# A three-layer float32 block on one core: earlier weight splits, rotary partners in partition halves, and a half-spectrum Fourier transform

## The chip, the cores and the metric

One core of one Trainium2 chip runs the whole program. The metric is the device time of one execution in microseconds, here the median of several runs.

## The reference

The input is x (1 x 512 x 1024, float32). The first layer projects the normed x into many parts and runs two attentions side by side: a sparse one (an indexer scores all earlier keys, the best 128 of each query are kept, softmax over those) and one with a forget gate. Both are gated and projected, merged by sigmoid weights and added to x. Then comes an "even" layer and an "odd" layer, both modulated by a condition vector, the first also over 256 context rows. The parts that the change touches are these:

```
def axial_rope(x, row, col):            # even layer: queries and keys, heads of 2 x 32 features
    half = x.shape[-1] // 2; nf = half // 2
    def rotate(u, pos):
        ang = pos[:, None] * inv_freq
        u1, u2 = u[..., :nf], u[..., nf:]
        return concatenate([u1 * cos - u2 * sin, u2 * cos + u1 * sin], axis=-1)
    return concatenate([rotate(x[..., :half], row), rotate(x[..., half:], col)], axis=-1)

def fourier_mix(u):                     # odd layer: 8 groups of 64 features
    ug = u.reshape(B, N, 8, 64)
    return fft2(ug, axes=(1, 3), norm='ortho').real.reshape(B, N, 512)
```

## The kernel before

The activations lie with features on the partitions, 128 of them by 512 tokens. Each operand of a large product is split into a high part (cast to fp32r) and a low part, and each product is made of three: high x high, high x low, low x high. The weights come as a stream of units (128 x 512) in granules of four (1 MB). SyncE loads a granule into one of two raw buffers (`w_raw`, line 1347) and, before it loads the next into the same buffer, waits until both parts of the old one exist. ScalarE casts each unit to its high part (`high(u)`, line 1371), in an order written out by hand: `high(upto)` casts all units up to that one, and waits for each until TensorE has read the unit that lay in the same place (there are four places, `ROOM`). GpSimd subtracts to get the low part (line 1194). TensorE waits for both (`tiles`, line 645). `ahead(chunk)` casts up to three units past the end of a chunk. Every engine runs its own program in order, so a wait holds back all that stands behind it.

The eight PSUM banks are dealt out by a pool: `next_bank` takes the next bank of the current tuple `pool[0]` and waits until its last reader has given it back. Small guest products (`modulate`, line 715) and their turned rows (`turn_due`, line 729) take banks in the same way; VectorE's `modulation` (line 2232) reads and frees the latter.

The stages that the change touches, in order of time:

- **keys, qi, qa (14 to 79 us).** After the keys' two tiles are copied, ScalarE computes the forget gate (lines 1456 to 1464: Abs, Exp, Ln with table loads and waits for VectorE), and only then goes on with `ahead("qi")`. After qi and qa it copies the four qa tiles (line 1469) and then splits the first index query (`prep_i(0)`: ScalarE line 1425, VectorE line 2122), for which the first index score (line 784) waits.
- **ga, gb, vb (135 to 219 us).** VectorE picks the best 128 keys in 16 rounds of `max` and `match_replace` (lines 2175, 2178), then frees gb's banks in `gated("gb")` (line 2165), then runs `modulation(0, (0, 1))`. The banks of gb are 5, 6, 7 and 4; its guest takes 2 and its turned row 3. The pool of vb is (0, 1, 2, 5, 6, 7), so vb's fourth tile takes bank 5.
- **After the attention, mb0, mb1 (349 to 403 us).** ScalarE casts the attention results (lines 1591, 1595) with one or more `high` between each two, runs the eight sigmoids of the merge gate (line 1599), and then the sigmoids that free mb0's banks (line 1606), the first of which mb1's third tile needs.
- **The even layer's queries and keys (632 to 709 us).** The partner of each feature is made by a permutation product (`rotate`, line 773, eight products in plain float32) between the units of e_v; VectorE's `rope` multiplies by the cosine (line 2086), the PSUM partner by the sine (line 2088) and adds (line 2090), in the order query 0, key 0, query 1, key 1 and so on. SyncE then stacks the parts of each head by 24 copies inside SBUF for the first two heads (line 1257), and `score_even` (line 987) waits for them.
- **The Fourier part (1299 to 1345 us).** The product with the sequence transform (`dft`) gives cosine columns 0 to 256 and sine columns 1 to 255. ScalarE copies each tile in two pieces (lines 1965, 1966), VectorE mirrors both (lines 2583, 2584), and TensorE applies the feature transform to two full tiles of 512 columns for each of four j, adding in PSUM (lines 1165, 1166). VectorE multiplies by the gate (line 2589), ScalarE and VectorE split the result, ScalarE waits for all of it (`nix_lo` 8), issues four loads of x (lines 1973, 1974) and only then casts the fifth unit of oo0.

## Time and profile before

| what | value |
|---|---|
| median of 3 runs (lowest to highest) | 1370.41 us (1368.09 to 1373.72) |
| the profiled execution's own time | 1370.77 us |
| its span, first to last instruction | 1369.0 us |
| TensorE / VectorE / ScalarE / GpSimd busy | 94% / 49% / 45% / 34% |
| mean granted TensorE clock | 0.983 of full |
| chain that ended last, by engine | PE 72%, DVE 11%, ACT 8% |

Busy shares are averages over the span. The times of an order in time are from the span's start; "[4.47 <-POOL w_low L1194]" says that the engine sat idle for 4.47 us before this row until that instruction released it. "x4" merges four instructions into one row.

### The profile page before, as it was taken

To read this page: it belongs to the slowest core of one execution; us is meant where nothing else is said; L and a number is where in the kernel's file an instruction comes from. 1 tells how busy PE (TensorE), PEld (TensorE's weight loads), DVE (VectorE), ACT (ScalarE), POOL (GpSimd) and SP (SyncE) were. 2 spreads that over 40 slices of the span, in tenths; PEclk is the share of its full clock that TensorE was granted. 3 is DMA by queue.
4 is the path that set the end of the run, shared out by engine and by line. 5 is a ranking of instruction groups with operands and counts; after the bars stand their busy time and mean duration, and the time that the engine had idled before them with its cause. 6 is when DMAs were issued, how large, how long until landed. Compare 5 with 4: busy or idle time off the path is not lost.

```text
span 1369.0 us, 19570 instructions
## 1 busy us (share of the span) xinstructions
PE 1286.5 (94%) x7164; PEld 1001.5 (73%) x7164; DVE 672.0 (49%) x1279; ACT 622.8 (45%) x1336; POOL 459.3 (34%) x360
## 2 busy tenths in 40 slices
PE   7899999999999998869999999999988999999998
PEld 6677766676678776668777887787867878677776
DVE  4466974665503342273268668623704601565343
ACT  7434325655432334262146666645325422655533
POOL 4534343221343443360133333331351133231341
PEclk9999999999999999989999999999999999999999
DMA  6331442000441544341052430001153232121452
GB/s 222 101 100 62 147 161 93 32 32 32 139 154 62 207 189 158 123 160 41 31 152 73 107 101 32 32 32 63 62 200 113 87 127 89 62 93 62 154 148 68
DMA packets 28685, 140.46 MB, mean 103 GB/s; under 512 B 4304, under 2 KB 5968, under 8 KB 15984
## 3 DMA queue, kind: packets, MB, share of 16 engines
q1 hardware_dynamic: 21840, 117.85, 25.5%
q10 hardware_dynamic: 6752, 21.35, 4.7%
q8 instruction: 60, 0.98, 0.3%
q14 instruction: 33, 0.27, 0.1%
HBM read 122.87 MB, written 6.29 MB: 94 GB/s over the span
## 4 chain that ended last, share of the span: by engine, by line
PE 72%; DVE 11%; ACT 8%; issue 3%; DMA 3%; POOL 3%; ACTq 1%; DVEq 0%; POOLq 0%; SPq 0%
PE psum L645 46%; PE psum L673 5%; DMA w_raw<-stream 2%; PE psum L784 2%; POOL w_low L1194 2%; DVE arena L2178 2%; PE psum L1011 2%; PE psum L1179 2%; DVE small L2175 2%; PE psum L875 2%; ACT w_high L1371 2%; PE psum L633 1%; PE psum L995 1%; DVE arena L2028 1%; PE psum L861 1%
## 5 line engine op out<-in xcount | busy, mean ns | idle before, releaser
L1194 POOL TENSOR_TENSOR w_low<-w_raw,w_high 128x512 fp32r<-128x512 f32 x264 | 353.4, 1352 | 733.2 <-ACT w_high L1371 733.0
L1371 ACT CAST w_high<-w_raw 128x512 fp32r<-128x512 f32 x264 | 158.1, 621 | 335.5 <-PE psum L645 183.7
L645 PE MATMUL psum<-x_high,w_high 128*128 128x512 f32 x528 | 224.5, 425 | 13.3 <-POOL w_low L1194 6.8
L645 PE MATMUL psum<-x_low,w_high 128*128 128x512 f32 x528 | 209.8, 397 | 0.0
L645 PE MATMUL psum<-x_high,w_low 128*128 128x512 f32 x528 | 209.6, 397 | 0.0
L645 PEld LDWEIGHTS psum<-x_high,w_high 128*128 128x128 f32 x528 | 99.9, 189 | 59.1 <-issue 23.8
L645 PE MATMUL psum<-w_high,x_high 128*128 128x512 f32 x288 | 120.0, 417 | 14.7 <-ACT w_high L1371 6.2
L645 PEld LDWEIGHTS psum<-x_high,w_low 128*128 128x128 f32 x528 | 99.9, 189 | 24.1
L645 PE MATMUL psum<-w_low,x_high 128*128 128x512 f32 x288 | 115.4, 401 | 0.0
L645 PE MATMUL psum<-w_high,x_low 128*128 128x512 f32 x288 | 115.2, 400 | 0.0
L645 PEld LDWEIGHTS psum<-x_low,w_high 128*128 128x128 f32 x528 | 100.3, 190 | 17.8 <-issue 0.7
L645 PEld LDWEIGHTS psum<-w_high,x_high 128*128 128x128 f32 x288 | 55.3, 192 | 40.1 <-issue 15.8
L2404 DVE TENSOR_REDUCE small<-psum 128x1 f32<-128x768 f32 (+1 forms) x96 | 69.9, 770 | 19.7 <-PE psum L987 19.6
L1731 ACT ACTIVATE arena<-psum,small 128x768 f32<-128x768 f32 (+1 forms) x84 | 63.3, 761 | 16.8 <-DVE small L2404 16.6
L1740 ACT COPY arena<-psum 128x512 f32<-128x512 f32 (+1 forms) x80 | 36.7, 459 | 68.2 <-PE psum L995 67.5
L1223 POOL TENSOR_SCALAR arena<-arena,small 128x768 f32<-128x768 f32 (+1 forms) x48 | 40.3, 840 | 79.1 <-DVE small L2411 79.1
L645 PEld LDWEIGHTS psum<-w_high,x_low 128*128 128x128 f32 x288 | 55.0, 191 | 13.6
L645 PEld LDWEIGHTS psum<-w_low,x_high 128*128 128x128 f32 x288 | 55.4, 192 | 12.9 <-issue 1.0
L673 PE MATMUL psum<-x_high,w_high 128*128 128x512 f32 x96 | 42.2, 440 | 0.5 <-DVE arena L2397 0.5
L2416 DVE SCALAR_TENSOR_TENSOR arena<-arena,small 128x768 f32<-128x768 f32 (+1 forms) x36 | 30.1, 835 | 18.9 <-POOL arena L1223 18.9
L673 PE MATMUL psum<-x_high,w_low 128*128 128x512 f32 x96 | 37.9, 395 | 0.0
L673 PE MATMUL psum<-x_low,w_high 128*128 128x512 f32 x96 | 37.9, 395 | 0.0
(456 smaller groups left out, 2688.5 us busy)
## 6 DMA issues: line engine op xcount, KB each, us to landing
w_raw<-stream SPq DMA_DIRECT2D x98, 1024.0 KB, 4.9
x_kept<-arena ACTq DMA_DIRECT2D x8, 512.0 KB, 4.5
arena<-x_kept ACTq DMA_DIRECT2D x8, 512.0 KB, 5.7
arena<-bias ACTq DMA_DIRECT2D x8, 512.0 KB, 3.7
q_masked<-e_q_high SPq DMA_DIRECT2D x24, 96.0 KB, 2.2
arena<-x SPq DMA_DIRECT2D x4, 512.0 KB, 5.2
arena<-x ACTq DMA_DIRECT2D x4, 512.0 KB, 7.4
arena<-ctx ACTq DMA_DIRECT2D x4, 512.0 KB, 6.8
```

Of the source, the lines that this page charges most:

```text
L645: mm = pe.matmul(o, l, r, start=(first and n == 0 and kind != "fc"), stop=(last and n == len(passes) - 1))
L673: mm = pe.matmul(o, l, r, start=k == 0 and n == 0, stop=k == NK - 1 and n == 2)
L784: mm = pe.matmul(acc, q[rows, :], k[rows, :], start=n == 0, stop=not more and n == 2)
L875: mm = pe.matmul(acc[64 * hh:64 * hh + 64, 0:P], v, A_PT[:, 2 * (d % 2) + hh, P * kt:P * kt + P], start=kt == 0, stop=kt == t)
L1011: mm = pe.matmul(acc[64 * hh:64 * hh + 64, 0:P], E_V[:, kt, 64 * head:64 * head + 64], E_PT[:, 2 * (d % 2) + hh, P * kt:P * kt + P], start ...
L1194: pool.tensor_tensor(PLACE[u][1], RAW[:, g % 2, u % 4, :], PLACE[u][0].bitcast(F32), ALU.subtract).then_inc(w_lo, 1)
L1223: pool.tensor_scalar(second, second, SM[:, RINV + c + 1:RINV + c + 2], SM[:, 82:83], ALU.mult, ALU.mult)\
L1371: act.copy(PLACE[u][0], RAW[:, g % 2, u % 4, :]).then_inc(w_hi, 1)
L1731: frees(act.activation(map_place(s, m), PS[:, 512 * b:512 * b + w], ACT.Exp, bias=scr(NEGMAX + c), accum_out=scr(ROWSUM + c)), key)
L1740: frees(act.copy(E_PT[:, 2 * (d % 2) + hh, P * c:P * c + w], ps[:, 0:w]), key)
L2404: dve.tensor_reduce(scr(NEGMAX + 2 * (s % 4) + m), PS[:, 512 * b:512 * b + w], AX.X, ALU.max, negate=True).then_inc(sig("e_neg"), 1)
L2416: dve.scalar_tensor_tensor(e0, e0, scr(RINV + c), e1, ALU.mult, ALU.add).then_inc(sig("e_p"), 1)
```

## The change

In the first layer ScalarE's splits are put in another order, `modulation(0, (0,))` moves into VectorE's selection loop and one pool changes. In the even layer the weight columns of e_q and e_k are laid out anew so that a feature and its partner lie 64 partitions apart; the permutation products go, VectorE makes the partner by two multiplications of 64 partitions each that write to the other half, all queries come before all keys, and the 96 stacking copies read every fourth partition instead of 32 neighbours. In the odd layer the feature transform is applied to 257 and 255 columns, each in its own part of a bank, and the sum and the mirror come after it.

```
-SQ = {n: i for i, n in enumerate(("ident", "causal", "perm_a", "perm_e", "ones_blk", "dft_c", "dft_s"))}
+SQ = {n: i for i, n in enumerate(("ident", "causal", "ones_blk", "dft_c", "dft_s"))}
...
+    for n in ("e_q", "e_k"):
+        chunks[n] = chunks[n].reshape(D, 4, 2, 2, 2, 2, 8).transpose(0, 1, 5, 4, 6, 2, 3).reshape(D, 512)
...
-        ROPE_E = [(t, (c, j)) for j in range(4) for t, c in ((E_Q[:, j, 0:S], "e_q"), (E_KF[:, j, :], "e_k"))]
+        ROPE_E = [(t[:, j, 0:S], (c, j)) for t, c in ((E_Q, "e_q"), (E_KF, "e_k")) for j in range(4)]
...
-        N_F = arena(4096, 8, S)
+        N_F = arena(4096, 4, S)
+        N_T = arena(6144, 4, S)
+        N_ODD = TAB.rearrange("p a (b n) -> p (a b) n", b=2)
```

On TensorE:

```
-            pool[0] = (0, 1, 2, 5, 6, 7)
+            pool[0] = (0, 1, 2, 3, 5, 6)
             gemm("vb", X)
...
                 unit("e_v", k, X, C)
-                if k < 4:
-                    pool[0] = (3, 0)
-                    rotate("rope_e", ROPE_E[2 * k:2 * k + 2], "perm_e", 2 * k)
...
             for j in range(4):
-                pe.wait_ge(sig("dft_whole"), j + 1)
+                consumed(pe, ("dft", j))
                 acc = next_bank(("fmix", j))
-                pe.matmul(acc[:, :], square("dft_c"), N_F[:, j, :], start=True, stop=False)
-                fills_bank(pe.matmul(acc[:, :], square("dft_s"), N_F[:, 4 + j, :], start=False, stop=True),
+                pe.matmul(acc[:, 0:HALF + 1], square("dft_c"), N_F[:, j, 0:HALF + 1], start=True, stop=True)
+                fills_bank(pe.matmul(acc[:, HALF + 1:S], square("dft_s"), N_F[:, j, HALF + 1:S], start=True, stop=True),
```

On SyncE:

```
-                    rows = slice(64 * hh + 32 * m, 64 * hh + 32 * m + 32)
-                        src = part[rows, pr, :]
+                        src = part[2 * hh + m::4, pr, :]
```

On ScalarE:

```
                 frees(act.copy(A_KF[:, i, :], ps[:, :]), ("keys", i))
+            high(UNITS["qi"][5])
             act.wait_ge(sig("f_in"), 1)
...
                 ahead(c)
+                if c == "qa":
+                    prep_i(0)
                 for j in range(4):
...
-            prep_i(0)
...
                 act.copy(BH[:, j, :], A_QA[:, j, :]).then_inc(sig("oa_hi"), 1)
-                high(next_unit + j)
+            high(next_unit + 1)
...
                 act.copy(CHA[:, j, :], A_QB[:, j, :]).then_inc(sig("ob_hi"), 1)
-                high(next_unit + 4 + j // 2)
+            high(next_unit + 2)
...
                 act.activation(MA[:, j, :], MA[:, j, :], ACT.Sigmoid).then_inc(sig("ma_out"), 1)
-                high(next_unit + 6 + j // 4)
+                if j == 3:
+                    high(next_unit + 3)
...
             ahead("e_k")
+            for j in range(4):
+                consumed(act, ("e_q", 4 + j // 2))
+                act.wait_ge(sig("rope_e_out"), j + 1)
+                act.copy(E_QH[:, j, :], E_Q[:, j, :]).then_inc(sig("q_high"), 1)
...
             for j in range(4):
-                consumed(act, ("e_q", 4 + j // 2))
-                act.wait_ge(sig("rope_e_out"), 2 * j + 1)
-                act.copy(E_QH[:, j, :], E_Q[:, j, :]).then_inc(sig("q_high"), 1)
-                act.wait_ge(sig("rope_e_out"), 2 * j + 2)
+                act.wait_ge(sig("rope_e_out"), 4 + j + 1)
                 act.copy(KH[:, j, L:L + S], E_KF[:, j, :]).then_inc(sig("ke_hi"), 1)
...
                 ps = filled(act, ("dft", j))
-                act.copy(N_F[:, j, 0:HALF + 1], ps[:, 0:HALF + 1])
-                frees(act.copy(N_F[:, 4 + j, 1:HALF], ps[:, HALF + 1:S]), ("dft", j))
+                frees(act.copy(N_F[:, j, :], ps[:, :]), ("dft", j))
+            for j in range(4):
+                ps = filled(act, ("fmix", j))
+                act.copy(N_ODD[:, j, 0:HALF - 1], ps[:, HALF + 1:S]).then_inc(sig("odd_out"), 1)
             high(UNITS["oo0"][3])
             for j in range(4):
-                consumed(act, ("fmix", j))
+                act.wait_ge(sig("fmix_g"), j + 1)
```

On VectorE:

```
-                dve.tensor_tensor(q, r[:, 0, :], r[:, 1, :], ALU.add).then_inc(sig(f"{name}_out"), 1)
+            def rope_e(i):
+                q, src = ROPE_E[i]
+                swapped = E_R[:, i % 2, :]
+                consumed(dve, src)
+                if i >= 2:
+                    dve.wait_ge(sig("rope_e_out"), i - 1)
+                for to, of in ((half_of(0), half_of(1)), (half_of(1), half_of(0))):
+                    dve.tensor_tensor(swapped[to], q[of], TAB[of, 1, :], ALU.mult).then_inc(sig("rope_e_part"), 1)
+                dve.wait_ge(sig("rope_e_part"), 3 * i + 2)
+                dve.tensor_tensor(q, q, TAB[:, 0, :], ALU.mult).then_inc(sig("rope_e_part"), 1)
+                dve.wait_ge(sig("rope_e_part"), 3 * i + 3)
+                dve.tensor_tensor(q, q, swapped, ALU.add).then_inc(sig("rope_e_out"), 1)
...
                 if n == 8:
                     gated("ga", GA)
+                if n == 12:
+                    modulation(0, (0,))
...
-            modulation(0, (0, 1))
+            modulation(0, (1,))
...
+            for j in range(4):
+                rope_e(j)
+                if j:
+                    low_query(j - 1)
+            low_query(3)
+            for j in range(4):
+                rope_e(4 + j)
+                if j:
+                    low_key(j - 1)
+            low_key(3)
...
             for j in range(4):
-                dve.memset(N_F[:, 4 + j, 0:S:HALF], 0.0)
+                ps = filled(dve, ("fmix", j))
+                dve.wait_ge(sig("odd_out"), j + 1)
+                whole, even, odd = N_T[:, j, :], ps[:, 0:HALF + 1], N_ODD[:, j, 0:HALF - 1]
+                dve.tensor_copy(whole[:, 0:S:HALF], even[:, 0:HALF + 1:HALF]).then_inc(sig("dft_part"), 1)
+                dve.tensor_tensor(whole[:, 1:HALF], even[:, 1:HALF], odd, ALU.add).then_inc(sig("dft_part"), 1)
+                frees(dve.tensor_tensor(whole[:, HALF + 1:S], even[:, HALF - 1:0:-1], odd[:, HALF - 2::-1], ALU.subtract),
+                      ("fmix", j))
+                dve.wait_ge(sig("dft_part"), 2 * j + 2)
+                consumed(dve, ("fmix", j))
+                dve.wait_ge(sig("gd_g"), j + 1)
+                dve.tensor_tensor(in_columns(N_Y[:, j, :]), in_columns(N_GD[:, j, :]), by_column(whole), ALU.mult)\
+                   .then_inc(sig("fmix_g"), 1)
...
```

## Rows read from the trace of the kernel before

**Rows 1.** The page: busy time and share of the engines.

```profile
PE 1286.5 (94%) x7164; PEld 1001.5 (73%) x7164; DVE 672.0 (49%) x1279; ACT 622.8 (45%) x1336; POOL 459.3 (34%) x360
```

**Rows 2.** What TensorE waited for, 0 to 400 us: total, times, longest.

```profile
PE psum L645 <- POOL w_low L1194: 5.0, 2, 4.5
PE psum L645 <- DVE gate_b L2165: 3.1, 1, 3.1
...
PE psum L645 <- ACT arena L1606: 2.3, 1, 2.3
```

**Rows 3.** A stretch after a stall: busy time, clock, DMA share, GB/s.

```profile
40.00:43.40 3.40, 3.29 (x8) 2.65 (x9) 3.37 (x3) 0.17 (x1) 3.40 (x3) 0.51 0.66 210
```

**Rows 4.** TensorE in order of time, 13 to 48 us.

```profile
40.11 0.77 PE L645 MATMUL psum<-x_high,w_high 128*128 128x512 f32 x1 [4.47 <-POOL w_low L1194]
```

**Rows 5.** ScalarE in order of time, 28 to 44 us.

```profile
30.11 0.63 ACT L1456 ACTIVATE arena<-arena 8x512 f32<-8x512 f32 x1 [0.54 <-DVE arena L2063]
...
38.00 2.18 ACT L1371 CAST w_high<-w_raw 128x512 fp32r<-128x512 f32 x4
```

**Rows 6.** TensorE, ScalarE and VectorE in order of time, around 80 us.

```profile
80.68 0.50 PE L784 MATMUL psum<-b_high,q_masked 64*128 64x256 f32 x4 [1.96 <-issue]
...
76.65 2.70 ACT L1469 ACTIVATE arena<-psum 128x512 f32<-128x512 f32 x4
...
77.39 1.67 DVE L2101 TENSOR_TENSOR arena<-arena 128x512 f32<-128x512 f32 x1
79.88 1.29 DVE L2122 TENSOR_TENSOR q_masked<-arena,q_masked 128x512 fp32r<-128x512 f32 x2 [0.83 <-ACT q_masked L1425]
```

**Rows 7.** TensorE and VectorE in order of time, around 195 us.

```profile
195.17 0.51 PE L645 MATMUL psum<-w_high,x_high 128*128 128x512 f32 x1 [3.14 <-DVE gate_b L2165]
...
194.43 2.48 DVE L2165 TENSOR_TENSOR gate_b<-gate_b,psum 128x512 f32<-128x512 f32 x4
```

**Rows 8.** TensorE and ScalarE in order of time, around 376 us.

```profile
378.44 0.50 PE L645 MATMUL psum<-x_high,w_high 128*128 128x512 f32 x1 [2.31 <-ACT arena L1606]
...
368.58 0.62 ACT L1371 CAST w_high<-w_raw 128x512 fp32r<-128x512 f32 x1 [5.95 <-DMA w_raw<-stream]
...
377.82 2.03 ACT L1606 ACTIVATE arena<-psum 128x512 f32<-128x512 f32 x4
```

**Rows 9.** The chain in order of time, 664 to 700 us: start, us, what.

```profile
672.73 1.72 PE psum L773 x4
674.44 4.19 PE psum L645 x18
```

**Rows 10.** VectorE lines 2086 and 2088: duration in ns, minimum, median, maximum.

```profile
L2086 DVE TENSOR_TENSOR arena<-arena,tables_sb x8: 692/692/1780, 645.4 to 695.5; 128x512 f32<-128x512 f32 x8
...
L2088 DVE TENSOR_TENSOR arena<-psum,tables_sb x8: 691/692/694, 673.7 to 696.2; 128x512 f32<-128x512 f32 x8
```

**Rows 11.** VectorE line 2435, two shapes: duration in ns, minimum, median, maximum.

```profile
L2435 DVE TENSOR_TENSOR e_conv_in<-e_conv_in,psum x8: 416/550/683, 734.0 to 886.8; 128x512 f32<-128x512 f32 x4, 128x256 f32<-128x256 f32 x4
```

**Rows 12.** SyncE's queue and TensorE in order of time, 685 to 710 us.

```profile
685.45 1.21 SPq L1257 DMA_DIRECT2D b_both<-k_high  x2
...
700.57 0.59 SPq L1257 DMA_DIRECT2D q_masked<-e_q_high  x1
...
708.81 0.40 PE L987 MATMUL psum<-b_both,q_masked 96*128 96x256 f32 x2
```

**Rows 13.** The chain in order of time, 1285 to 1369 us.

```profile
1310.98 0.86 PE psum L1165 x2
...
1317.85 22.40 PE psum L645 x96
```

**Rows 14.** ScalarE, its queue and GpSimd in order of time, 1309 to 1326 us.

```profile
1309.18 0.38 ACT L1966 COPY arena<-psum 128x255 f32<-128x255 f32 x1
...
1321.09 1.91 ACTq L1973 DMA_DIRECT2D arena<-x_kept  x3
...
1324.50 3.79 POOL L1194 TENSOR_TENSOR w_low<-w_raw,w_high 128x512 fp32r<-128x512 f32 x3 [10.97 <-ACT w_high L1371]
```

100 lines of the change are left out of this document (34 added, 66 removed).

## The prediction

> **What bounds the kernel.** The page comes first: TensorE is busy for 1286.5 of 1369.0 us, 94%, and no other engine reaches half [rows 1]. So a microsecond is saved where a product goes or where TensorE stands still, and work on another engine counts only where TensorE waits for it. The second view is the list of what TensorE waited for. In the first 400 us it names three single waits that the change touches: GpSimd's low part of a weight (4.5 us), a bank held by VectorE's gate (3.1 us) and a bank held by ScalarE's sigmoid (2.3 us) [rows 2]. The timelines around them show who is late and why, and the chain shows the removed products themselves. Everything after a stage is coupled by the weight ring, so I let later stages move with TensorE and keep their own stalls.
>
> **Part 1, the early split in qi.** TensorE stands 4.47 us at 40.11 us for the low part of unit qi[3] [rows 4]. ScalarE casts that unit only at 38.00, after the forget gate's run that begins at 30.11, 7.9 us [rows 5]. Its place has been free since about 27 us (TensorE stopped at 40.11 - 4.47 = 35.6, three units of 12 products at 0.233 us after it, from 18 products in 4.19 us [rows 9]). With the cast of qi[3] to qi[5] ahead of the forget gate, qi[3] is there in time. The price: qi[5] goes into the place of qi[1], which TensorE leaves one unit before it stopped, at 32.8. So the forget gate starts at 33.3 and ends at 41.2, and then comes the cast of qi[6], whose low part is ready near 43.3 to 44.2. TensorE, unstalled, wants it at 35.6 + 3 x 2.8 = 44.0. I charge 0.3 us. The work queued behind this on ScalarE (the qi casts) is hidden by TensorE's 2.8 us a unit.
>
> The stall has a second price. The granted clock in the 3.4 us after it is 0.51, the 1.2 GHz level, and 8 products take 3.40 us, 0.425 each [rows 3], where at 2.4 GHz they take 0.233 [rows 9]: 8 x 0.192 = 1.5 us. It fell after the idle of 4.47 us and goes with it. Part 1: 4.5 + 1.5 - 0.3 = 5.7 us; bounds 3 (the stall returns at qi[6] by 1.5 us and keeps the slow clock) and 6.0.
>
> **Part 2, the first index query.** TensorE stands 1.96 us at 80.68 [rows 6]. ScalarE copies four qa tiles from 76.65 to 79.3 and only then splits the query; VectorE ends its rope at 79.06, waits 0.83 us for that cast, and subtracts from 79.88 on [rows 6]. With the split first, VectorE goes on at 79.1: gain 0.8 us. VectorE's rope is late next. The copies move by one cast of 0.6 us; what waits for them (the swap of qa, whose rope runs inside the index stage) has that stage as cover. Bounds: 0, and 0.8 + 1.5 if a slow stretch like that of part 1 follows this gap too and vanishes, which I don't count.
>
> **Part 3, vb's banks.** TensorE stands 3.14 us at 195.17, since vb's fourth tile takes bank 5, which `gated("gb")` frees from 194.43 on [rows 7]. The new pool gives banks 0 to 3 to vb, and bank 5 to the guest product after two units. TensorE is there at 192.0 (where it stopped) + 15 x 0.233 = 195.5; the bank is free at 194.43 + 2.48 / 4 = 195.05, plus 0.2 for the `modulation` that moved into the selection loop ahead of it. Bank 3 holds the turned row that this `modulation` frees long before. Gain 3.1 us, with a margin of only 0.2 us. Bounds 2.0 and 3.3. The weights follow: vb[4] needs its raw granule only after two more units.
>
> **Part 4, the merge gate.** TensorE stands 2.31 us at 378.44 for the sigmoid of line 1606, which starts at 377.82 because ScalarE lost 5.95 us at 368.58 to a load, with four attention casts and eight merge sigmoids behind it [rows 8]. In the new order no unit beyond mb0[7] is cast before the eight sigmoids end. They are as short as line 1606's, about 0.55 us each (four in 2.03 us), and wait for nothing that is late, so they are over before the load lands at 368.6, and the sigmoid follows mb0's end at once: 378.44 - 2.31 less the 6 products of mb1's first two tiles, 374.7. Gain 2.3 us. The casts of mb0[4] to mb0[7] come up to four casts of 0.6 us later; each has three units, 8.4 us, between its place coming free and its use, so these cost nothing. The next granule slips by a microsecond with them; mb1[0] is wanted at 374.7, 6 us after it lands. Bounds 0 and 2.3.
>
> **Part 5, the permutation products.** Four pairs between the e_v units, each 1.72 us of the chain [rows 9]: 6.9 us, all on TensorE while it never waits. What replaces them must be done before `score_even` starts, at 708.81 before [rows 12] and 702 after. VectorE's old rope is three instructions of 0.69 us [rows 10], the new one four; I take 64 partitions as the same 0.69 us, since the length along a row is unchanged. The queries' four are made from 645 us on, under the e_k products where VectorE was idle; the keys' take 4 x (4 x 0.73 + 0.7) = 14.5 us from about 668 on (708.8 less the products and eight units of 4.19 us [rows 9]), with low parts, and end near 683. SyncE's 24 copies began at 685.45 and the last was issued at 700.57, 0.63 us each [rows 12]; they can now begin after the second key rope and its low part, at about 675 and end at 690, 12 us before they are wanted. All this is free, for it lies under the 33.6 us of e_v products; without that cover it would cost its 14.5 us.
>
> The product from PSUM took 692 ns at most 694, while line 2086, with both inputs in SBUF, took up to 1780 ns for the same shape [rows 10], each time with a GpSimd instruction running. The change makes all four instructions of a rope such as line 2086. If each of the 16 for the keys took 1.78 us, the keys' ropes would end at 668 + 16 x 1.78 + 4 x 0.7 = 699, SyncE could still begin after the second of them, at 683, and be done at 698: the sum stays. Part 5: 6.9 us; bounds 5 and 6.9.
>
> **Part 6, the Fourier part.** Eight products of 0.86 us run from 1310.98 to 1317.85 [rows 13]. With half the columns they take half: 3.4 us less on TensorE. ScalarE's two copies of 0.38 become one of 0.65 and VectorE's mirror goes, both hidden. But the chain behind grows. For each j, ScalarE copies 255 odd elements (0.38 [rows 14]), VectorE makes a copy of two elements (some 0.1, my estimate), a sum and a difference (0.42 each, by the 128 x 256 form of line 2435 [rows 11]) and the gated product (0.69 [rows 10]): 1.8 us with the waits. Four of them from 1312.4 end at 1319.6, and four low parts at the spacing of 0.62 us (as in 2.48 for four [rows 7]) at 1322.1, or later where GpSimd runs, instead of 1321.05. ScalarE waits for the last of them, then issues the loads (from 1321.09) and casts oo0[4]; GpSimd's low part starts at 1324.50 [rows 14] and takes 1.3 us. So that part is ready at 1326.8 to 1327.4 (0.6 us is half of what line 2086 lost at its longest [rows 10]; the gated product now has both inputs in SBUF and GpSimd runs once beside these four), and TensorE, 3.4 us earlier, wants it at 1314.4 + 48 x 0.233 = 1325.6. A wait of 1.5 us takes the place of what was hidden. The last granule is paced by the same low parts and is still ahead of TensorE, as is line 1179's first use. Part 6: 3.4 - 1.5 = 1.9 us; bounds 0.5 and 3.4.
>
> The Trainium skill (SBUF — State Buffer, section Who interferes with whom) speaks against this part: a VectorE instruction with two SBUF inputs contends with a GpSimd instruction that reads SBUF, one with a PSUM input doesn't. By it one gated product would lose the full 1.1 us between 1.78 and 0.69, the wait would be 1.3 + 1.1 = 2.4 us, part 6 1.0 us, and the time 0.9 us longer, 1350.6. Rows 10 agree as far as they go: 1780 ns at the longest against 694.
>
> **The sum.** 5.7 + 0.8 + 3.1 + 2.3 + 6.9 + 1.9 = 20.7 us. Against the profiled execution, whose own time is 1370.8 us, that is 1350.1; the median of the runs is 0.4 us lower, so I predict 1349.7 us. The lower bounds add to 10.5 us, the upper to 24.5.
>
> **Rivals.** (a) Gains given back: a front stall returns elsewhere, above all the one of part 1 at qi[6], where I have a margin of half a microsecond, or that of part 4 at the next granule; with parts 1 to 4 at half (6 us) and 5 and 6 in full the time is 1370.4 - 14.8 = 1355.6. For it: hand-set orders have one late unit hidden behind another. Against: each successor in the timelines has 0.3 to 5 us to spare. (b) Only TensorE's work counts, and the stalls of parts 1 to 4 all move to the next wait: 6.9 + 1.9 give 1361.6. Against it: the clock drop of 1.5 us goes with the longest stall in any case. (c) Better: part 6 keeps 3.4 us and the slow clock of part 2 goes: 1370.4 - 23.5 = 1346.9. (d) Slower than before: the stacking copies. They read every fourth partition, and no row of this trace shows such a source. SyncE has 702 - 675 = 27 us for 24 of them, 1.1 us each; above that `score_even` waits. The whole gain is used up by a stall of 20.7 us, at 2.0 us a copy; at 2.5 us the first 24 end 33 us late and the time is at least 1370.4 - 20.7 + 33 = 1383. For it: unseen form. Against: same bytes, same rows, 32 runs either way. The Trainium skill (SBUF — State Buffer, section Door 1: The DMA port swizzle) maps partitions to ports so that every fourth partition reaches all ports and 32 neighbours only half; by it a copy is no slower. (e) The change does nothing where it says: no; the products leave the program, so at least part 5 shows.
>
> **How the numbers follow.** Forecast (1345.5 to 1353): 0.58. Rival (a), 1353 to 1359: 0.25. Rival (b), 1359 to 1364: 0.07. Rival (c), below 1345.5 with runs that scatter by 3 us: 0.06. Rival (d): 0.02, the rest 0.02 near no change. The range 1343.5 to 1358.5 holds 0.85 of it before my own errors of sizing, and takes in all but the lowest bounds. Half a percent, 6.9 us, is about what a measurement of this kernel can tell from no change. Faster by more, below 1363.6: 0.94; within: 0.04; slower: 0.02.
>
> **What would show it.** In the changed profile: no wait of TensorE for a low part near 36 us, and no clock below full there; under 1.5 us before the first line 784; no wait for `gate_b` near 185; none for line 1606 near 365; no line 773, and copies of 0.6 us in SyncE's queue; fmix's matmuls at half their time, with a new wait of 1 to 2 us of TensorE for a low weight four units into oo0. I am wrong if a TensorE wait of over 2 us stands in the list that was not there before, or if the copies issue or land more slowly.

## The result, and the profile after the change

| | before | after |
|---|---|---|
| median of 4 runs (lowest to highest) | 1372.07 us (1368.09 to 1377.16) | 1349.31 us (1347.97 to 1352.08) |
| span of the profiled execution | 1369.0 us | 1346.2 us |
| its own time | 1370.8 us | 1348.0 us |

The ratio is 0.9827, 95% interval 0.9804 to 0.9849: 1.7% faster, by 22.8 us in the medians and in the spans. Forecast were 20.7 us. (The kernel before was run once more beside the changed one, so its median here is 1.7 us above the one that the forecast was counted from.)

The page and TensorE's wait list for 0 to 400 us (total, times, longest) answer to [rows 1, 2]:

```profile
PE 1273.7 (95%) x7148; PEld 995.7 (74%) x7148; DVE 681.2 (51%) x1287; ACT 625.1 (46%) x1336; POOL 460.9 (34%) x360
```

```profile
PE psum L785 <- DVE arena L2036: 7.4, 1, 7.4
PE psum L774 <- issue: 2.0, 2, 1.0
...
PE psum L642 <- POOL w_low L1181: 0.5, 1, 0.5
```

TensorE is busy for 12.8 us less, though the products that go are only 6.9 and 3.4 us. The other 2.5 us fit less work at the slow clock (its mean is 0.986 against 0.983). The three long waits of [rows 2] are not there. (The code moved up by some lines: 645 is now 642, 784 is 774, 1371 is 1357, 1194 is 1181.)

ScalarE in order of time, 28 to 41 us, and around 70 us [rows 5, 6]:

```profile
28.62 1.28 ACT L1357 CAST w_high<-w_raw 128x512 fp32r<-128x512 f32 x2
32.03 0.62 ACT L1357 CAST w_high<-w_raw 128x512 fp32r<-128x512 f32 x1 [2.12 <-PE psum L642]
32.56 0.63 ACT L1443 ACTIVATE arena<-arena 8x512 f32<-8x512 f32 x1
...
40.45 1.66 ACT L1357 CAST w_high<-w_raw 128x512 fp32r<-128x512 f32 x3
...
69.38 0.62 ACT L1411 CAST q_masked<-arena 128x512 fp32r<-128x512 f32 x1
69.91 2.35 ACT L1462 ACTIVATE arena<-psum 128x512 f32<-128x512 f32 x4
```

The three casts stand ahead of the forget gate, which begins at 32.56 and lets the next cast start at 40.45, and behind its first weight product at 13.87 us TensorE has no gap above 0.53 us up to 72.67. There it still stands 1.04 us, where it stood 1.96.

The rope's new line on VectorE (minimum, median, maximum in ns) and SyncE's copies with the first even score, in order of time [rows 10, 12]:

```profile
L2085 DVE TENSOR_TENSOR arena<-arena,tables_sb x16: 684/686/1672, 630.0 to 665.4; 64x512 f32<-64x512 f32 x16
```

```profile
660.17 1.18 SPq L1243 DMA_DIRECT2D b_both<-k_high  x2
...
674.76 0.59 SPq L1243 DMA_DIRECT2D q_masked<-e_q_high  x1
...
686.56 0.40 PE L974 MATMUL psum<-b_both,q_masked 96*128 96x256 f32 x2
```

The last copy is issued 11.8 us before the score. Half the partitions take the same 0.69 us (the two of the 16 that took 1.67 us, at 632.93 and 634.63, ran beside GpSimd), and TensorE reaches the score without a wait.

The Fourier part, VectorE and ScalarE, GpSimd and TensorE in order of time [rows 13, 14]:

```profile
1291.00 1.06 DVE L2594 TENSOR_TENSOR arena<-arena 128x512 f32<-128x512 f32 x1
1291.98 0.16 DVE L2587 COPY arena<-psum 128x2 f32<-128x2 f32 x1
1292.05 0.42 DVE L2588 TENSOR_TENSOR arena<-psum,tables_sb 128x255 f32<-128x255 f32 x1
1292.38 0.42 DVE L2589 TENSOR_TENSOR arena<-psum,tables_sb 128x255 f32<-128x255 f32 x1
...
1294.81 1.29 DVE L2594 TENSOR_TENSOR arena<-arena 128x512 f32<-128x512 f32 x1
...
1297.92 2.49 DVE L2025 TENSOR_TENSOR x_low<-arena,x_high 128x512 fp32r<-128x512 f32 x4
...
1300.44 1.91 ACTq L1965 DMA_DIRECT2D arena<-x_kept  x3
1302.38 0.62 ACTq L1966 DMA_DIRECT2D arena<-x_kept  x1
1303.11 2.18 ACT L1357 CAST w_high<-w_raw 128x512 fp32r<-128x512 f32 x4 [4.44 <-issue]
...
1293.18 1.97 POOL L1181 TENSOR_TENSOR w_low<-w_raw,w_high 128x512 fp32r<-128x512 f32 x1 [5.23 <-ACT w_high L1357]
1303.87 5.03 POOL L1181 TENSOR_TENSOR w_low<-w_raw,w_high 128x512 fp32r<-128x512 f32 x4 [8.72 <-ACT w_high L1357]
...
1305.28 0.47 PE L642 MATMUL psum<-w_high,x_high 128*128 128x512 f32 x1 [1.91 <-ACT w_high L1357]
```

This is the chain that the prediction named: VectorE's low parts, four issues, the cast of oo0[4], its low part, a wait of TensorE. The last row names a cast of ScalarE as what ended the wait. It is the fourth of that run, which ended at the same moment; the cast of oo0[4] was over at 1303.73, and its low part on GpSimd, for which TensorE waits too, ran from 1303.87 to 1305.14. The gated product (line 2594) is the surprise: 1.06 us or more, where 0.69 was assumed. In the kernel before the same product (line 2589) read its columns from PSUM:

```profile
1312.81 0.69 DVE L2589 TENSOR_TENSOR arena<-arena,psum 128x512 f32<-128x512 f32 x1 [0.61 <-PE psum L1166]
```

### The profile page after: what moved, and what is told of

The parts are those of the page before. It is cut to its first block and busy times, and to the rows that moved or that the text cites. A ratio compares the mean times of both kernels' runs of the same rounds, so it can differ in the third digit from the quotient of the medians.

```text
span 1346.2 us, 19533 instructions
## 1 busy us (share of the span) xinstructions
PE 1273.7 (95%) x7148; PEld 995.7 (74%) x7148; DVE 681.2 (51%) x1287; ACT 625.1 (46%) x1336; POOL 460.9 (34%) x360
```

## The experiments

The runs of one kernel scatter by 3 to 9 us, more than most parts are worth. So each profile is cut at instructions that occur in all of them, and the stretches between are compared. The stretches are: **A** from the first weight product to the first index score; **B** from there to the first wait for a bank of the index stage (102.19 us in the changed kernel); **C** from the last guest product of ga (160.27) to the first score with the keys (207.00); **D** from the last wait of the attention (335.94) to the weight wait in bb (474.50); **E** from there to the merge's transposes (598.08); **F** from there to the second product of the even attention (687.50); **G** from there to the wait for the converter's low part (1277.25); **H** from there to the end. All in us, from the start times of TensorE's rows:

| kernel | A | B | C | D | E | F | G | H | span |
|---|---|---|---|---|---|---|---|---|---|
| before | 65.96 | 31.05 | 50.15 | 141.03 | 124.73 | 96.23 | 589.76 | 69.49 | 1369.0 |
| changed | 58.80 | 29.52 | 46.73 | 138.56 | 123.58 | 89.42 | 589.75 | 68.95 | 1346.2 |
| changed_again | 58.79 | 29.54 | 46.72 | 140.31 | 123.79 | 90.35 | 591.12 | 68.81 | 1351.0 |
| undo_qi | 64.85 | 29.55 | 46.73 | 139.40 | 127.11 | 89.62 | 589.86 | 68.77 | 1357.0 |
| undo_prep | 59.73 | 29.53 | 46.74 | 138.91 | 124.19 | 89.09 | 590.57 | 68.18 | 1346.9 |
| undo_pool | 58.80 | 29.54 | 51.67 | 138.59 | 124.99 | 90.39 | 591.09 | 68.98 | 1354.5 |
| undo_mb0 | 58.79 | 29.54 | 46.73 | 142.94 | 123.75 | 89.34 | 589.80 | 68.11 | 1350.9 |
| undo_perm | 58.78 | 29.54 | 46.73 | 138.99 | 126.93 | 96.40 | 590.11 | 68.10 | 1355.0 |
| undo_fmix | 58.82 | 29.55 | 46.74 | 140.22 | 126.29 | 89.28 | 591.48 | 69.42 | 1353.5 |
| early_cast | 58.80 | 29.55 | 46.73 | 140.53 | 125.29 | 89.61 | 588.00 | 70.09 | 1350.3 |
| in_psum | 58.80 | 29.55 | 46.73 | 141.31 | 124.71 | 89.54 | 589.95 | 66.88 | 1349.2 |
| in_psum_again | 58.79 | 29.53 | 46.73 | 139.52 | 124.48 | 89.41 | 589.86 | 66.51 | 1346.3 |

The two not in it (flat_read, old_rows) agree in A to C within 0.03 us. Where their code is the same, A, B and C repeat to 0.04 us; D to H scatter by 1 to 4 us, where TensorE waits for loads and its clock then drops or not. The scatter sits in a few places. From 358.06 to 443.23 us (inside D) and from 620.2 to 687.50 us (inside F), counted in the changed kernel, the same stretches between the same instructions repeat to 0.05 us as well, and they are used below.

Two stretches lie between those of the table. From B to C is 58.08 us in all, within 0.02. From C to D (207.00 to 335.94) takes 127.80 us before and 128.94 changed: after idles of 0.57 and 0.91 us around 331 us the clock falls to 0.50 in the changed kernel (332 to 334 us) and stays at 1.00 in the kernel before (345 to 347 us), and the other profiles, with the same code there, take either 127.8 or 128.5 to 129.0 us. So the first pair hides a loss of 1.1 us that the change did not cause.

The kernel before was run beside each group of experiments, with medians of 1373.88, 1374.23 and 1375.49 us, so medians of different groups can be compared only by their ratios to it. The spans that were expected of the runs with one part changed, all counted from the changed kernel's 1346.2 us, came out 2.0 to 6.7 us too low (that of undo_prep 0.3 us too high): 1346.2 was the shortest span of all.

**What repeats (changed_again, 5 runs).** No edit.

> The changed kernel once more, to tell what in a profile repeats. Theory: the stretches up to 330 us and from 600 us on repeat within 0.3 us, and those between, where TensorE waits for loads and the clock drops, scatter by 1.5 us each; the first product comes anywhere from 13.5 to 14.9 us. So the gain of 22.8 us of span shown by the first pair of profiles is within 3 us of what any pair would give: the span is 1346 to 1351, the ratio to the kernel before 0.981 to 0.985. Rival (each run's stretches differ freely): no stretch repeats within 0.5 us.

Median 1352.82 us against 1373.88 of the kernel before on the same chip, ratio 0.985 (0.983 to 0.9871). The theory holds for A, B and C, and in this pair for H; F and G differ by 0.9 and 1.4 us, more than expected. The first profile of the changed kernel was a lucky one: its D of 138.56 and its E of 123.58 are the shortest of all. The two pairs of medians give 22.8 and 21.1 us for the change; 20.7 to 23.4 us lies inside both intervals.

**Part 1 undone (undo_qi, 4 runs).**

```
             frees(act.copy(A_KF[:, i, :], ps[:, :]), ("keys", i))
-            high(UNITS["qi"][5])
             act.wait_ge(sig("f_in"), 1)
```

> The changed kernel without the early split of qi[3] to qi[5] ahead of the forget gate. Theory (that stall and the slow clock behind it were taken away by this line alone, and nothing later gave it back): TensorE stands 4.5 us for qi[3]'s low part near 39.2 us, 8 products behind it at half speed, 1.5 us; the forget gate's cast chain is no longer ahead of qi[6]. Time 5.5 to 6 us over the changed kernel: a span of 1352. Rival (gain given back later): the later stages have slack that takes it up, 1348 to 1350.

1357.95 us, ratio 0.9876 (0.9854 to 0.9897). The wait is back, with a slow clock behind it (TensorE's row, and the stretches with their clock after the busy times):

```profile
39.68 0.77 PE L642 MATMUL psum<-x_high,w_high 128*128 128x512 f32 x1 [4.47 <-POOL w_low L1181]
```

```profile
39.60:41.00 1.40, 1.32 (x3) 1.16 (x4) 1.40 (x2) 0.15 (x1) 1.40 (x1) 0.50 0.48 70
41.00:43.00 2.00, 2.00 (x7) 1.53 (x7) 1.97 (x2) 0.00 (x0) 2.00 (x3) 0.58 0.82 328
43.00:45.00 2.00, 2.00 (x10) 1.64 (x9) 0.45 (x1) 0.62 (x1) 1.80 (x2) 1.00 0.36 147
```

Stretch A is 64.85 - 58.80 = 6.05 us longer and B and C are unchanged: the gain is that of this line, and nothing up to 330 us takes it back. Behind that the stretches scatter too much to tell: the span is 1357.0 us, 10.8 above the first changed profile and 6.0 above the second.

**Part 2 undone (undo_prep, 4 runs).** `prep_i(0)` stands behind the four qa copies again.

> The changed kernel with the first index query's split behind the four qa copies again, as before. Stretches are taken between the same instructions in each profile. From the first weight product to the index stage's first product the kernel before takes 65.96 us, the changed one without the early qi split 64.85, the changed one 58.80. Theory (the split costs VectorE a wait of 0.83 us, and TensorE's idle of 1.96 us has a slow clock behind it, while the one of 1.04 us has none): this stretch takes 59.7 to 59.9 us with an idle of 1.96 us at its end, and the next one, to the first wait for a bank of the index stage, 31.05 us instead of 29.52. Rival (the slow clock behind 1.96 us was chance): the second stretch stays at 29.5. The whole: 1 to 2.5 us over the changed kernel.

1351.09 us, ratio 0.9831 (0.9809 to 0.9854). TensorE's row and the stretches behind it:

```profile
73.78 0.50 PE L774 MATMUL psum<-b_high,q_masked 64*128 64x256 f32 x4 [1.97 <-issue]
```

```profile
73.70:75.00 1.30, 1.22 (x9) 1.02 (x10) 0.75 (x2) 0.39 (x1) 0.00 (x0) 1.00 0.49 63
75.00:77.00 2.00, 2.00 (x10) 1.60 (x9) 0.18 (x1) 0.00 (x0) 0.00 (x0) 1.00 0.44 90
```

Here are the same stretches of the kernel before, after the idle of 1.96 us:

```profile
80.60:82.00 1.40, 1.32 (x8) 1.02 (x9) 0.79 (x2) 0.38 (x1) 0.00 (x0) 0.66 0.55 76
82.00:84.00 2.00, 2.00 (x6) 1.57 (x5) 0.14 (x1) 0.00 (x0) 0.00 (x0) 0.50 0.36 78
```

A grows by 0.93 us as expected, but B does not: the clock stayed at the 2.4 GHz level behind an idle as long as the one that was followed by 1.2 GHz before. The rival holds. The 1.5 us of B are not part 2's.

**Part 3 undone (undo_pool, 4 runs).**

```
-            pool[0] = (0, 1, 2, 3, 5, 6)
+            pool[0] = (0, 1, 2, 5, 6, 7)
             gemm("vb", X)
```

> The changed kernel with the old bank pool for vb (0, 1, 2, 5, 6, 7), the early modulation of part 0 kept. Theory (the bank that the gate frees was the wait, and the pool took it away): TensorE stands 3.1 us for gate_b at about 185.6 us again, and the time is 3.1 to 3.5 us over the changed kernel: a span of 1349.3 to 1349.7. Rival (the wait vanishes anyway since the gate now comes earlier against TensorE, or it is given back at the next load): under 1.5 us.

1354.99 us, ratio 0.9858 (0.9831 to 0.9885). TensorE's row, and a stretch of this kernel behind it:

```profile
186.35 0.68 PE L642 MATMUL psum<-w_high,x_high 128*128 128x512 f32 x1 [3.12 <-DVE gate_b L2164]
```

```profile
187.30:188.30 1.00, 1.00 (x4) 0.81 (x3) 0.78 (x2) 0.00 (x0) 0.00 (x0) 0.50 0.98 418
```

and of the kernel before, one microsecond after the wait of [rows 7]:

```profile
196.00:197.00 1.00, 1.00 (x6) 0.82 (x5) 0.99 (x3) 0.00 (x0) 0.00 (x0) 1.00 0.99 418
```

The wait is the expected one, but C is 4.94 us longer, beyond the 3.1 to 3.5 us of the theory. Between the kernel before and the changed one it differs by 3.42 us (50.15 - 46.73): 3.14 of idle, and 0.28 because TensorE's products, 0.23 us apart, take up again behind it with a start-to-start distance of 3.52 and one of 0.34 us. The other 1.5 us are clock: behind nearly the same wait eight products start 0.43 us apart here and 0.23 us apart in the kernel before. So 3.4 us is what the part took away; whether the 1.5 us of clock come with this kernel or with this one execution stays open.

**Part 4 undone (undo_mb0, 4 runs).** ScalarE casts a unit behind each attention cast and each sigmoid again.

> The changed kernel with ScalarE's old order around the merge gate (a cast behind each attention cast and behind each sigmoid). Theory: ScalarE loses some 6 us to a load with the sigmoids behind it, TensorE stands 2.3 us for mb0's first sigmoid near 364 us: span 1348.5. Rival (the ring of weights decides: the trace of the changed kernel shows this part's gain of 1.8 us lost again by 501 us and back by 613 us, so loads take it up): within 1 us of the changed kernel's 1346.2.

1352.08 us, ratio 0.9842 (0.9817 to 0.9867). ScalarE in order of time, and TensorE:

```profile
359.39 0.62 ACT L1357 CAST w_high<-w_raw 128x512 fp32r<-128x512 f32 x1 [5.85 <-DMA w_raw<-stream]
...
368.63 2.03 ACT L1594 ACTIVATE arena<-psum 128x512 f32<-128x512 f32 x4
...
369.25 0.50 PE L642 MATMUL psum<-x_high,w_high 128*128 128x512 f32 x1 [2.22 <-ACT arena L1594]
```

In the changed kernel the merge gate's eight sigmoids end before the load (these are the last four), and those that free the bank come behind it without delay:

```profile
351.84 2.20 ACT L1587 ACTIVATE merge_a<-merge_a 128x512 f32<-128x512 f32 x4
358.22 1.15 ACT L1357 CAST w_high<-w_raw 128x512 fp32r<-128x512 f32 x2 [4.18 <-DMA w_raw<-stream]
...
360.83 2.70 ACT L1595 ACTIVATE arena<-psum 128x512 f32<-128x512 f32 x4
```

The wait returns to the place and size of the theory. D is 142.94 us against 138.56 to 141.31 in the ten other kernels of the table that have the new order; 141.03 before. That is above all of them, but D scatters by as much as the part is worth. The stretch inside it from 358.06 to 443.23 us doesn't: it takes 85.12 to 85.17 us in the twelve kernels with the new order, 87.61 here and 87.73 before. So the part is worth 2.4 to 2.6 us, and 80 us later none of it has been given back.

**Part 5 undone (undo_perm, 4 runs).** Everything of the change but the rope: old columns, eight permutation products, old stacking source and order.

> The kernel before with every part of the change except the rope without permutation products (old weight columns, permutation squares, old stacking source and order of ropes). Theory (eight products of 0.86 us on TensorE with nothing else late): 6.8 us over the changed kernel: a span of 1353.0, from TensorE's work alone; score_even starts with 0.2 us of wait or none in both. Rival A (the changed rope frees VectorE and SyncE too): more than 7.5 us. Rival B (part is hidden): under 5 us. A side question: this kernel loads six more 64 KB squares' worth less two, that is seven squares where the changed one loads five; the changed kernel's first weight product starts at 13.87 us, the kernel before's at 14.72. If the larger load is the cause, it starts at 14.7 here; if not, at 13.9.

1358.62 us, ratio 0.9881 (0.9861 to 0.99). F takes 96.40 us, as in the kernel before (96.23), against 89.09 to 90.39 without the products; seven of those ten lie between 89.28 and 89.62, 6.8 to 7.1 us below. From 620.2 to 687.50 us it is sharper: 67.27 us in all twelve without the products, 74.12 in the two with them, so the part is worth 6.85 us and nothing there is hidden or freed besides. The span is 2.0 us above the expected 1353.0, most of it in E, which scatters (126.93 us here). By the ratios the whole differs from the changed kernel by 4 to 7 us. The side question is settled too: with seven squares of 64 KB loaded the first weight product starts at 13.54 us, with five at 14.65 (undo_fmix) or 13.87 (changed). The start is chance, and so is the 0.85 us that the first pair shows there.

**Part 6 undone (undo_fmix, 4 runs).** Mirror, full products and product from PSUM as in the kernel before.

> The changed kernel with the old Fourier part: whole spectrum by VectorE's mirror, eight products of 512 columns, gated product from PSUM. Theory (the removed products were paid back behind them): the changed kernel's trace has fmix 3.4 us shorter, but then TensorE stands 1.9 us for unit oo0[4] at 1305.28 and 0.3 us at 1322.07, and its slower start of the last weights costs the rest, so undoing it costs only 0.6 us: a span of 1346.8 against 1346.2. By the prediction's own term it would cost 1.9 us, 1348.1. Rival (TensorE's work counts in full and the waits at 1305 and 1322 were there for another reason): 3.4 us, 1349.6, and both waits stay.

1351.36 us, ratio 0.9829 (0.9807 to 0.9851), equal to the changed kernel. H is 69.42 us (69.49 before) against 68.10 to 68.98 in the eight profiles with the new Fourier part as it is (seven of the table, and old_rows with 68.73): the part is worth 0.4 to 1.3 us, 0.8 to 0.9 in the mean, and both waits of the changed kernel's tail are absent here.

The spread of those eight has a cause that the traces show. All eight stand 1.90 to 1.93 us at oo0[4]. SyncE issues the last granule of weights 31.7 us after the start of H in all of them, but it lands 37.0 to 37.5 us after that start in three (undo_prep, undo_mb0, undo_perm), where TensorE meets no further wait and H is 68.1 to 68.2 us, and 38.7 to 38.9 us after it in five, where TensorE waits 0.3 us at oo1 and has lost 0.7 us by the time that it is through. ScalarE's first cast of that granule, changed kernel (38.8 us after H's start) and undo_mb0 (37.5):

```profile
1316.09 2.19 ACT L1357 CAST w_high<-w_raw 128x512 fp32r<-128x512 f32 x4 [8.71 <-DMA w_raw<-stream]
```

```profile
1320.27 1.66 ACT L1357 CAST w_high<-w_raw 128x512 fp32r<-128x512 f32 x3 [7.35 <-DMA w_raw<-stream]
```

So the part is worth 1.3 us where the granule lands early and 0.4 to 0.8 us where it lands late. What decides the landing was not tried.

**A cast moved ahead of the loads (early_cast, 4 runs).**

```
                 act.copy(XH[:, 4 + j, :], N_Y[:, j, :]).then_inc(sig("nix_hi"), 1)
+                if j >= 2:
+                    high(UNITS["oo0"][2 + j])
```

> The changed kernel with one thing moved: ScalarE casts oo0[4] and oo0[5] right behind the third and fourth feature casts, ahead of its wait for all low parts and of its four load issues (2.7 us from 1300.44). Theory (the wait of 1.91 us at 1305.28 comes from ScalarE's queue: oo0[4]'s place is free at about 1295 and its raw weights are there): the wait goes, the last granule comes as much earlier since GpSimd starts two low parts earlier, span 1344.0 to 1344.5. Rival A (the last granule, which lands at 1316, paces the end): the wait moves to oo1, span 1345.7 to 1346.2. Rival B (ScalarE waits for the place or the raw weights in front of the feature casts): the feature casts come later and the low parts with them, no gain or a loss of up to 1 us.

1350.94 us, ratio 0.983 (0.981 to 0.985), and H is 70.09 us, 1.1 longer. The wait at oo0[4] is gone, but none of the theories named all that came. VectorE's four low parts, GpSimd's beside them, and TensorE, in order of time:

```profile
1300.89 4.71 DVE L2027 TENSOR_TENSOR x_low<-arena,x_high 128x512 fp32r<-128x512 f32 x4
...
1300.38 3.46 POOL L1181 TENSOR_TENSOR w_low<-w_raw,w_high 128x512 fp32r<-128x512 f32 x2 [2.27 <-ACT w_high L1357]
...
1321.89 0.47 PE L1166 MATMUL psum<-w_high,x_high 128*128 128x512 f32 x1 [1.61 <-ACT w_high L1357]
```

The low parts took 4.71 us where they take 2.49 in the changed kernel: the two that overlap GpSimd's instructions took 1.8 us each, the two behind them 0.68. ScalarE waits for them, so its loads are 2.2 us late (counted from the start of H) and the casts behind them 1.7 us. The last granule is issued 0.2 us late and lands 0.7 us late. As in rival A the wait moved to oo1, 1.61 and 0.30 us, together 0.3 us less than the two waits of the changed kernel. That H is longer all the same is the clock, in this profile and not in the changed kernel's:

```profile
1323.30:1325.50 2.20, 2.20 (x6) 1.28 (x5) 2.07 (x3) 2.12 (x6) 2.17 (x2) 0.51 0.00 0
```

```profile
1320.00:1339.70 19.70, 19.38 (x82) 14.85 (x80) 8.60 (x15) 5.73 (x16) 1.92 (x2) 1.00 0.25 81
```

Eight products 0.43 us apart instead of 0.23 are about 1.5 us. Without them H would be some 68.6 us (an estimate), the mean of the changed kernel: the moved cast gains nothing, and this one profile does not show that it costs anything.

**The column read told apart (flat_read, 1 run).**

```
-                ... in_columns(N_GD[:, j, :]), by_column(whole), ALU.mult)
+                ... in_columns(N_GD[:, j, :]), in_columns(whole), ALU.mult)
```

> The changed kernel, but the gated product reads the whole spectrum straight, element after element, instead of by columns (the feature mix's output is then permuted, so this part of the computation is changed). Theory (the column stride of a read from SBUF costs the extra): four gated products of 0.69 us, except one that runs beside GpSimd. Rival (two inputs in SBUF cost it, whatever the stride): 1.07 us as before. The span follows: 1344.5 to 1345 by the first, 1346.2 by the second.

The gated product in ns, minimum, median, maximum:

```profile
L2594 DVE TENSOR_TENSOR arena<-arena x4: 691/693/1002, 1294.1 to 1299.0; 128x512 f32<-128x512 f32 x4
```

With the straight read it takes 0.69 us, and 1.00 once, beside GpSimd. In the changed kernel it took 1.06 to 1.10 and 1.29. So the column stride costs 0.38 us and GpSimd 0.2 to 0.3 us. In both kernels GpSimd's instruction overlaps two of the four products, and only the one that starts after it is slowed. In the changed kernel the one that started before it (1292.89 us) took 1.10 us, and GpSimd's own instruction took 1.97 us, where it takes 1.30 us in flat_read. H is 67.42 us.

**The spectrum made in PSUM (in_psum 4 runs, in_psum_again 5 runs).**

```
+                dve.tensor_tensor(ps[:, HALF + 1:S], even[:, HALF - 1:0:-1], odd[:, HALF - 2::-1], ALU.subtract) ...
...
+                dve.tensor_tensor(even[:, 1:HALF], even[:, 1:HALF], odd, ALU.add) ...
...
+                dve.tensor_tensor(in_columns(N_Y[:, j, :]), in_columns(N_GD[:, j, :]), by_column(ps), ALU.mult)
```

> The changed kernel with the whole spectrum made in PSUM: VectorE writes the difference over the odd half of the bank (ScalarE has copied it), adds the odd part to the even half in place, and the gated product reads the bank by columns as the kernel before did; the copy of two elements goes. Theory (the gated product takes 1.07 us instead of 0.69 because it reads SBUF by columns, one element of each 256 bytes): it falls to 0.69, a step of VectorE's chain from 1.93 to about 1.5 us, the last low part comes about 1.8 us earlier, and with it the wait of 1.91 us at 1305.28 nearly goes: span 1344.3 to 1344.8. Rival (the product's 0.38 us is a matter of GpSimd at work beside it or of its output): it stays above 1.0, and the span above 1345.5.

> The changed kernel with the whole spectrum made in PSUM, beside the changed kernel on the same chip. Its last stretch, from the last wait for the converter's low part to the end, was 66.88 us against 68.95. Theory: this repeats, and the median is 1.5 to 2.5 us below that of the changed kernel in the same rounds, about as much as the scatter of the runs. Rival (the 2 us are chance as well): the last stretch is 68 us or more and the medians are equal.

1350.04 us, 0.9828 (0.9809 to 0.9847), and 1351.28 us, 0.9825 (0.9799 to 0.9851), the second beside 1352.82 us of the changed kernel (changed_again). The same columns, read from the bank (VectorE in order of time, second run):

```profile
1295.70 0.42 DVE L2587 TENSOR_TENSOR psum<-psum,tables_sb 128x255 f32<-128x255 f32 x1
1296.16 0.43 DVE L2590 TENSOR_TENSOR psum<-psum,tables_sb 128x255 f32<-128x255 f32 x1
1296.63 0.69 DVE L2593 TENSOR_TENSOR arena<-arena,psum 128x512 f32<-128x512 f32 x1
1297.23 0.42 DVE L2587 TENSOR_TENSOR psum<-psum,tables_sb 128x255 f32<-128x255 f32 x1
```

A step takes 1.53 us instead of 1.93, no product is slower than another, and TensorE's longest wait in the Fourier part and after it is 0.2 us. H is 66.88 and 66.51 us, 1.9 to 2.4 us below the changed kernel's two (1.2 to 2.5 below the eight profiles with its Fourier part) and 2.5 to 2.9 below undo_fmix: most of the 3.4 us of removed products. The medians differ by 1.5 us in the same sense, within their scatter. It is the best version of the study by its profile, and by its median it can't be told from the changed kernel.

**The old stacking source (old_rows, 1 run).** `src = part[rows, pr, :]` with 32 neighbouring partitions.

> The changed kernel, but the stacking copies read 32 neighbouring partitions as in the kernel before instead of every fourth (the even attention then mixes dimensions of other heads, so this part of the computation is changed). Theory (the partitions' step costs nothing): copies of 0.59 us in SyncE's queue and about the same time to landing in both, no wait of TensorE at the first even score, same stretch of 89.4 us up to there. Rival (a step of four partitions costs or saves): copies or landings differ by over 20%.

The DMA lists between 660 and 700 us, KB each and median us to landing, first the changed kernel, then this one:

```profile
q_masked<-e_q_high SPq DMA_DIRECT2D x10, 96.0 KB, 2.6
```

```profile
q_masked<-e_q_high SPq DMA_DIRECT2D x8, 96.0 KB, 2.2
```

The issue takes 0.59 us in both. The landing takes 0.4 us longer with every fourth partition, on the 20% boundary that was set; the keys' copies (b_both<-k_high) land in 2.7 us against 2.1, beyond it. So the rival holds for the landing. The kernel before and undo_perm, the other two that read neighbours, land these copies in 2.2 us too. Nobody waits for them: TensorE reaches the score without a wait in both. F is 90.45 us here where 89.4 was expected, but the part of it from 620.2 us on takes 67.27 us as in the others.

## Why the prediction was right, step by step

The time was 0.4 us from the forecast, closer than its terms deserve. Part of that is luck: the gain was 2.1 us larger than forecast, and the median of the kernel before rose by 1.7. What each step said, and what the runs show:

| part | forecast | shown | by |
|---|---|---|---|
| 1 | 5.7 | 6.05 | A, undo_qi |
| 2 | 0.8 | 0.93 | A, undo_prep |
| 3 | 3.1 | 3.42 | C before and after |
| 4 | 2.3 | 2.4 to 2.6 | inside D, undo_mb0 |
| 5 | 6.9 | 6.85 | inside F, undo_perm |
| 6 | 1.9 | 0.4 to 1.3 | H, undo_fmix |
| slow clock in B | 0 | 1.5, cause open | B |
| sum | 20.7 | 21.6 to 22.7 | 22.8 and 21.1 in the medians |

The 22.8 us of the first pair also hold 0.85 us of an earlier start and 1.15 us in E, both chance, less the 1.1 us of slow clock around 333 us; none of these was a term of the forecast. (Its upper bounds add to 24.2 us, not 24.5; the range does not hang on it.)

Part 1 held in its mechanism too: the forget gate began at 32.56 us against a forecast 33.3, and the 0.3 us charged for qi[6] was not needed. The margin of half a microsecond on which rival (a) was built was enough. The stall's second price, 1.5 us of slow clock, was right: 6.05 less the idle of 4.47 leaves 1.58, of which 1.3 are the products at half speed and 0.3 the restart that part 3 shows too.

Part 2: as forecast. The 1.5 us kept as its upper bound did appear, in stretch B, but not for the reason given, since undo_prep has the same idle and no slow clock. None of the 13 other profiles has it, but of the kernel before there is only one, so whether an edit took it away stays open. Rival (c) is therefore half borne out, with a wrong cause.

Part 3: as forecast, 0.3 us more. The narrow margin at bank 5 was enough. The 0.3 is the restart behind the wait, which the sum, counting only idle time, left out.

Part 4: the order of events is that of the prediction, and no wait for line 1595 stands in the list. It was 0.1 to 0.3 us more than forecast and stood in full at 443 us. What survives to the end the runs can't tell, since D varies by 2.8 us in kernels that are the same there.

Part 5: right, 6.85 us of 6.9. Counted back from the first score, the keys' ropes run from 34.9 to 16.7 us ahead (forecast 34 to 19) and the copies are issued from 26.4 to 11.2 us ahead (forecast 27 to 12). Only the assumption that a copy from every fourth partition lands no later was wrong, by 0.4 us under 11 us of cover. So rival (d) fails: its limit was 1.1 us a copy, and it is 0.59.

Part 6 is the step that failed, by its size. The mechanism was the forecast one: the wait, its place, and the low part of oo0[4] as what ended it. The term "the gated product (0.69)" was mis-sized. It is 1.06 to 1.29 us, so a step of VectorE's takes 1.9 to 2.1 us and not 1.8, and the wait was 1.91 us instead of 1.5. The 0.69 came from the rope's products [rows 10], whose reads are straight; in the kernel before the gated product took 0.69 too, but read its columns from PSUM. The same read from SBUF costs more, which flat_read and in_psum show from both sides. With the restart, the wait cost 2.15 us of the 3.4, which leaves 1.3. A second step failed in five of the eight profiles: "the last granule [...] is still ahead of TensorE". There it lands 1.2 to 1.9 us later than in the other three, TensorE waits 0.31 us at oo1 and loses 0.7 us in all. The clock has no part in it: it stands at 1.00 behind that wait in the first profile. The Trainium skill (SBUF — State Buffer, section Who interferes with whom) gave 1.0 us for this part instead of 1.9, and the runs' mean is 0.9, but only in part for its reason: of the two products that ran beside GpSimd one lost 0.2 us by it, not 1.1, since it started only 0.3 us before GpSimd's instruction ended, and the other started first and lost nothing that can be told from the scatter. The rest is the stride and the late granule. The same page says, in its section on Door 1, that SBUF is read in lines of 16 bytes and that each step to a new line is paid for; with 256 bytes between elements the 0.38 us agree with it in kind. It gives no figure to compare. The same stride from PSUM cost nothing here (0.69 us).

Rival (b) is refuted by undo_qi, undo_prep, undo_pool and undo_mb0: each stall that went stayed away in the stretches that repeat. Rival (a) gave a higher time than any median of the changed kernel.

## What to carry to other kernels

When an operand moves from PSUM to SBUF, price the instruction again in its new access pattern, and not only for its neighbours: a strided read that was free from one memory cost half as much again from the other. A chain that waits for one engine's last result before it does unrelated work (here: four loads and a cast behind all low parts) was not cured by moving the cast alone, since that set another engine to work beside the ones it waits for, and the next wait took the gain. And when parts are smaller than the scatter of the runs, compare stretches between instructions that all profiles share. Where a stretch scatters, find the instruction at which the profiles part, and cut there: the 2.5 us of part 4 are lost in the scatter of D and plain in the 85 us inside it, which repeat to 0.05 us.

## What was not expected of the hardware

- **The clock after a stall is not given by the stall's length.** An idle of 1.96 us was followed by a granted clock of 0.50 in the kernel before and one of 1.97 us by 1.00 in undo_prep; 3.14 us by 1.00 before and 3.12 us by 0.50 in undo_pool; 0.91 us by 1.00 before and by 0.50 in the changed kernel. Each fall costs 1.1 to 1.5 us. Such falls are part of the scatter between profiles; how much of the 9 us between runs of one kernel they make up was not shown. What decides it is open: no run varied what goes before.
- **A column read in SBUF** (256 bytes from element to element, both inputs in SBUF) makes a product of 128 x 512 take 1.06 us instead of 0.69; the same columns from PSUM take 0.69. Whether a single strided input would also pay was not tried.
- **VectorE beside GpSimd:** four subtractions from SBUF took 4.71 us where they take 2.49 alone; a strided product lost 0.2 us, a straight one 0.3. Those slowed had started after GpSimd's instruction. A product that started 0.3 us before one took 1.10 us, hardly more than without, and GpSimd's instruction 1.97 us instead of 1.3.
- **Stacking copies from every fourth partition** of SBUF landed in 2.6 us, from 32 neighbours in 2.2. The Trainium skill (SBUF — State Buffer, section Door 1: The DMA port swizzle) lets 32 neighbours reach half of the ports and every fourth partition all, by which they should be no slower; here the measurement decides.
